# Value pages spread between past sums, later stores and states, a second home for the last value pages, and 4+4 output weight tiles in a hybrid decoder kernel

## The chip, the cores and the metric

The kernel runs as one launch on one core of a Trainium2 chip. TensorE (PE in the profile) multiplies and transposes, VectorE (DVE), ScalarE (ACT) and GpSimd (POOL) compute, and SyncE (SP) and GpSimd issue most of the transfers, which 16 DMA engines carry out. The metric is the device time of one execution in microseconds (us). Each engine runs its own instructions in the order written, and engines wait for each other through semaphores.

## The reference

Two layers over 256 prompt tokens and 64 sample tokens (8 sequences of 8 new tokens, each with 1024 past tokens in a paged cache of 128-token pages). The model width is 1024.

```python
def trunk(x, sample):
    for l in range(DEPTH):                       # 2 layers
        x = x + 0.5 * _swiglu(_rmsnorm(x, norm_ffn1_g[l]), ffn1_w_gate[l], ffn1_w_up[l], ffn1_w_down[l])
        o, rows = _token_mix(_rmsnorm(x, norm_mix_g[l]), w_in[l], ..., w_out[l], past)
        x = x + o
        x = x + 0.5 * _swiglu(_rmsnorm(x, norm_ffn2_g[l]), ffn2_w_gate[l], ffn2_w_up[l], ffn2_w_down[l])
    return _rmsnorm(x, norm_final_g)

def _token_mix(h, ...):
    qa, ka, va, qf, kf, vf, ff, qc, fc, ic, gc = jnp.split(h @ w_in, split_at, axis=-1)
    oa = _moba_attend(qa, ka_all, va_all, pos0)          # 6 heads: 256-key blocks, each query keeps its best 3
    of = _fox_attend(qf, kf_all, vf_all, lf_all, pos0)   # 5 heads: score + sum of log forget gates between
    oc, s_new = _hgrn2_recurrence(qc, kc, ic, logf_c, s0)    # 5 heads: linear recurrence with a state
    oc = _rmsnorm(oc, hgrn_g) * jax.nn.silu(heads(gc, C_HEADS))
    o = jnp.concatenate([oa, of, oc], axis=-1) @ w_out
```

The outputs are the new x, and for every layer the new keys, values, forget logs and states.

## The kernel before

All 320 tokens lie in the columns of the tiles. A layer goes through five stages: FFN1, input projection, a mix loop, the output projection and FFN2. In the dense stages (`dense`, PE line L1647) each float32 weight tile is split in two: ACT writes the high part (`hi`, L644), DVE the rest (`lo`, L956), and PE forms three products, x high by w high, x high by w low, x low by w high. Weights come into two raw buffers, "slots" 0 and 1, in turn.

The mix loop has 32 iterations a layer, i = 4q+n, one for each 256-key block n (two pages) of each sequence q. In iteration i, PE transposes the keys of block i+1 (`turn_keys`, L1864, 12 transposes into three PSUM banks that ACT and DVE copy out by turns) and multiplies block i's scores (`block_scores`, L1886). Once per sequence it adds, for the sequence before: at n=1 the transposed softmax weights (L1897, L1901), at n=2 the weighted values (`values`, L1913 to L1921), and at n=3 a transpose of their result (`turn_outputs`, L1929). In the gaps lie the prompt's own attention (i up to some 15), the levels of the recurrence (i=15 to 23) and from i=24 on (END0) its ends, states and root mean squares. After the loop stand these three steps for the last sequence, q=7.

Four queues feed the loop, each in a written order:

- SP loads key pages (two transfers a page, L510 and L511, four page slots that PE frees in turn), the recurrence's states (`load_states`, three transfers, L526) and stores new tokens (`store_tokens`, L519 and L520).
- POOL loads value pages (`load_values`, two transfers a page, L615 and L616), eight pages a sequence into one buffer, each once the sequence before has used that page. Between them it does `add_past` (L608), a copy of the summed forget logs behind the keys of a block; `turn_keys` of that block waits for it.
- ACT: copies of the key transposes (L778), exponentials (L788), softmax factors and scaled weights (`block_factors`, L804 to L815), copies of turned weights (L824), and in iteration 29 the recurrence's root mean squares (`rec_rstd`, L875 and L878, an Ln and an Exp, each with an ACT_TABLE_LOAD ahead). `block_factors` of q=0 waits for all ten stores of the new tokens.
- DVE: row maxima and gates (L1318 to L1330), key copies, norms, scaled outputs (`scale_outputs`, L1360), their copies into the mixed rows (`copy_outputs`, L1369 to L1372) and the recurrence.

The output projection takes its eight k-tiles in four chunk pairs, slot 0 with five tiles and slot 1 with three. ACT (hi), DVE (lo) and PE each wait for the one before them. After each pair DVE adds the product into x (`accumulate`), squares it (L970), adds the square up (L971) and forms the low part of the next x. Ahead of it, PE waits for `ol` (L1616), the low part of the mixed sample rows, which DVE forms behind `lo(0)` of the first chunk.

Of the kernel before, what the change touches and what calls it, by code (L numbers as in the profile page):

```python
# [33 lines left out]
ALU = mybir.AluOpType  # L34
# [219 lines left out]
def trunk(nc, a, outs):  # L254
    ctx = ExitStack()
    with ctx:
# [40 lines left out]
        value_pages = sb("value_pages", [128, NPG, AW + BW])  # L297
        sb("value_rest", [128, 18 * NT - NPG * (AW + BW)])
# [5 lines left out]
        pt = lambda n: P[:, n * NT:(n + 1) * NT]  # L304
        ROW_AT = [384 * n for n in (0, 2, 1, 3, 4)]
# [109 lines left out]
        out_tok, out_st = sem("out_tok"), sem("out_state")  # L415
# [22 lines left out]
        def _(sp):  # L438
# [21 lines left out]
            def wout_chunks(L, m):  # L460
# [3 lines left out]
                fill(0, u, [(raw[0][:, 0:5, :], rows(0, 640).rearrange("l (k p) n -> p (l k) n", p=128))])  # L464
                sp.wait_ge(split_done[1], u + 1)
                sp.dma_start(raw[1][0:64, 0, :], rows(640, 64).rearrange("l p n -> (l p) n")).then_inc(wout_in, 16)
                fill(1, u, [(raw[1][64:128, 0, :], rows(960, 64).rearrange("l p n -> (l p) n")),
                            (raw[1][:, 1:3, :], rows(704, 256).rearrange("l (k p) n -> p (l k) n", p=128))])
# [10 lines left out]
            for L in range(DEPTH):  # L479
# [33 lines left out]
                def store_tokens(groups):  # L513

                    for g in groups:
# [3 lines left out]
                        sp.dma_start(pv[:, ds(L * 2, 2), :], tokp[:, 0:2, g * 384:g * 384 + w]).then_inc(out_tok, 16)  # L519
                        sp.dma_start(sv[ds(L, 1), :, :].rearrange("l t c -> (l t) c"), toks[0:NS, g * 384:g * 384 + w]).then_inc(out_tok, 16)  # L520
# [12 lines left out]
                store_tokens(KEY_OUTS)  # L533
                sp.dma_start(outs["fox_logf_prompt"].rearrange("l b (n p) h -> p (l b n) h", p=128)[:, ds(L * 2, 2), :],
                             tokf[:, 0:2, :]).then_inc(out_tok, 16)
                sp.dma_start(outs["fox_logf_sample"].rearrange("l b t h -> l (b t) h")[ds(L, 1), :, :].rearrange("l t h -> (l t) h"),
                             tokf[0:NS, 2, :]).then_inc(out_tok, 16)
                for pg in range(6):
                    key_page(0, pg)
                load_states()  # L540
                sp.wait_ge(rows_copied_dve, L * 8 + 6)
                sp.wait_ge(rows_copied_act, L * 7 + 6)
                for pg, g in zip((6, 7), VALUE_OUTS):
                    key_page(0, pg)
                    store_tokens((g,))
                for q in range(1, DB):
                    for pg in range(NPG):
                        key_page(q, pg)

# [27 lines left out]
            sp.wait_ge(out_tok, 10 * 16 * DEPTH)  # L577
# [6 lines left out]
        def _(pool):  # L584
# [13 lines left out]
            for L in range(DEPTH):  # L598
# [1580 lines left out]
```

## Time and profile before

| | us |
|---|---|
| median of three runs | 1723.29 (1721.86 to 1725.35) |
| the profiled execution | 1721.82 |
| its span in the trace | 1720.1 |
| PE busy | 1608.1 (93%) |
| DVE busy | 1059.7 (62%) |
| ACT busy | 666.5 (39%) |

In the trace a layer's mix loop stands at 366 to 596 and 1207 to 1438 us, its output projection at 596 to 632 and 1438 to 1474. The number after a row's start is how long it took, xN counts the instructions put together in it, and brackets name the idle time before it and what ended that. PEclk is the granted clock of PE as a share of full speed.

### The profile page before, as it was taken

How to read it: one execution, taken by the hardware profiler on the slowest of the kernel's cores; microseconds unless marked ns; L12 is line 12 of the kernel's file. 1: busy time of each engine (PE TensorE's matmuls, PEld its weight loads, DVE VectorE, ACT ScalarE, POOL GpSimd, SP SyncE). 2: the span in 40 equal slices, each digit the busy share in tenths (PEclk: the TensorE clock that was granted, in tenths of full speed). 3: DMA queues.
4: the chain of work that ended last, by engine and by line, in shares of the span. 5: the costliest groups of instructions: out<-in, count | busy, mean ns of one | idle time of the engine just before them, and what ended most of it. 6: DMA issues, size and time to landing. Idle time of an engine off the chain costs nothing. (4 is left out here: it accounts for less than half of the span.)

```text
span 1720.1 us, 35333 instructions
## 1 busy us (share of the span) xinstructions
PE 1608.1 (93%) x13333; PEld 1492.0 (87%) x13333; DVE 1059.7 (62%) x1800; ACT 666.5 (39%) x969; POOL 160.6 (9%) x329
## 2 busy tenths in 40 slices
PE   6999999979989689999999999999799887999998
PEld 6999999966666489999999999999567666999997
DVE  6666557646576476665566665666556755766654
ACT  4333332436453443333343333425554442433323
POOL 0000000022424200000000000000233431000000
PEclk9999999989999799999999999999898997999999
DMA  6544455556757444444444444554766773544444
GB/s 199 155 154 153 136 152 131 147 188 206 236 180 242 146 147 147 146 147 139 154 156 153 153 141 143 157 143 121 226 211 206 218 216 120 170 153 150 140 141 141
DMA packets 282107, 282.34 MB, mean 164 GB/s; under 512 B 42894, under 2 KB 270918, under 8 KB 281862
## 3 DMA queue, kind: packets, MB, share of 16 engines
q1 hardware_dynamic: 266210, 234.28, 44.8%
q0 software_dynamic: 14464, 46.48, 8.5%
q8 instruction: 72, 1.18, 0.3%
q14 instruction: 45, 0.37, 0.1%
q10 hardware_dynamic: 1316, 0.03, 0.1%
HBM read 274.34 MB, written 6.40 MB: 163 GB/s over the span
## 5 line engine op out<-in xcount | busy, mean ns | idle before, releaser
L1647 PE MATMUL PS<-xh,whi 128*128 128x320 f32 x1840 | 576.0, 313 | 12.7 <-DVE xl L965 7.0
L1647 PE MATMUL PS<-xl,whi 128*128 128x320 f32 x1840 | 569.2, 309 | 0.0
L1647 PE MATMUL PS<-xh,wlo 128*128 128x320 f32 x1840 | 569.2, 309 | 0.0
L644 ACT ACTIVATE whi<-raw 128x2048 fp32r<-128x2048 f32 (+2 forms) x181 | 331.1, 1829 | 571.5 <-PE PS L1647 566.9
L956 DVE TENSOR_TENSOR wlo<-raw,whi 128x2048 fp32r<-128x2048 f32 (+2 forms) x181 | 395.3, 2184 | 235.2 <-ACT whi L644 233.0
L1647 PEld LDWEIGHTS PS<-xh,whi 128*128 128x128 f32 x1840 | 346.1, 188 | 15.9 <-DVE wlo L956 10.1
L1647 PEld LDWEIGHTS PS<-xh,wlo 128*128 128x128 f32 x1840 | 346.1, 188 | 1.5
L1647 PEld LDWEIGHTS PS<-xl,whi 128*128 128x128 f32 x1840 | 345.9, 188 | 0.0
L1647 PE MATMUL PS<-hh,whi 128*128 128x320 f32 x704 | 217.7, 309 | 0.0
L1647 PE MATMUL PS<-hl,whi 128*128 128x320 f32 x704 | 217.5, 309 | 0.0
L1647 PE MATMUL PS<-hh,wlo 128*128 128x320 f32 x704 | 217.5, 309 | 0.0
L1864 PE MATMUL PS<-K,key_pages 128*128 128x128 f32 x768 | 114.5, 302 | 50.7 <-POOL key_pages L608 21.5
L1864 PEld LDWEIGHTS PS<-K,key_pages 128*128 128x128 f32 x768 | 94.4, 155 | 65.9 <-issue 63.0
L778 ACT ACTIVATE keys_t<-PS 128x512 f32<-128x512 f32 x128 | 75.1, 595 | 151.8 <-PE PS L1864 151.7
L1647 PEld LDWEIGHTS PS<-hh,wlo 128*128 128x128 f32 x704 | 132.1, 188 | 0.0
L1647 PEld LDWEIGHTS PS<-hh,whi 128*128 128x128 f32 x704 | 132.1, 188 | 0.0
L1647 PEld LDWEIGHTS PS<-hl,whi 128*128 128x128 f32 x704 | 132.1, 188 | 0.0
L608 POOL COPY key_pages<-past 128x10 f32<-128x10 f32 x64 | 15.7, 250 | 1099.6 <-DVEq L951 953.6
L999 DVE TENSOR_TENSOR tmp<-PS,rstd 128x320 f32<-128x320 f32 x88 | 42.5, 487 | 88.8 <-PE PS L1647 88.7
L1303 DVE COPY keys_t<-PS 128x512 f32<-128x512 f32 x64 | 44.2, 691 | 76.0 <-PE PS L1864 72.3
L664 ACT ACTIVATE tmp<-tmp 128x320 f32<-128x320 f32 x88 | 40.3, 463 | 117.2 <-DVE tmp L999 117.1
L615 POOL DMA_DIRECT2D value_pages<-in_cache_moba_v x128 | 70.1, 547 | 151.7 <-issue 94.8
(262 smaller groups left out, 1793.6 us busy)
## 6 DMA issues: line engine op xcount, KB each, us to landing
raw<-in_ffn_w_gate SPq DMA_DIRECT2D x45, 1024.0 KB
raw<-in_ffn_w_up SPq DMA_DIRECT2D x45, 1024.0 KB
raw<-in_ffn_w_down SPq DMA_DIRECT2D x32, 1024.0 KB
key_pages<-in_cache_moba_k SPq DMA_DIRECT2D x128, 192.0 KB, 2.8
value_pages<-in_cache_moba_v POOLq DMA_DIRECT2D x128, 192.0 KB, 3.2
raw<-in_w_in SPq DMA_DIRECT2D x46, 512.0 KB
key_pages<-in_cache_fox_k SPq DMA_DIRECT2D x128, 160.0 KB, 3.5
value_pages<-in_cache_fox_v POOLq DMA_DIRECT2D x128, 160.0 KB, 3.8
```

Of the source, the lines that this page charges most:

```text
L608: pool.tensor_copy(key_pages[:, pg:pg + 2, AW + BW:AW + BW + BH], past_of[:, L, q, 2 * n:2 * n + 2, :]).then_inc(past_in, 1)
L615: pool.dma_start(value_pages[:, pg, 0:AW], vmv[:, ds(page + L * NPOOL, 1), :].rearrange("p a c -> p (a c)")).then_inc(v_in[pg], 16)
L644: act.activation(whi[s][:, 0:nk, 0:w], raw[s][:, 0:nk, 0:w], ACT.Copy).then_inc(hi_done[s], 1)
L664: act.activation(tmp[j][:, :], tmp[j][:, :], ACT.Silu).then_inc(silu_done, 1)
L778: act.activation(keys_t[i % 2][:, 4 * u:4 * u + 4, :], PS[:, bank, :].rearrange("p (j c) -> p j c", j=4), ACT.Copy).then_inc(read_act[bank ...
L956: dve.tensor_tensor(wlo[s][:, 0:nk, 0:w], raw[s][:, 0:nk, 0:w], whi[s][:, 0:nk, 0:w].bitcast(F32), ALU.subtract).then_inc(split_done[s], 1)
L999: dve.tensor_tensor(tmp[j][:, :], PS[:, j, 0:NT], rstd[:, :], ALU.mult).then_inc(gate_scaled, 1)
L1303: dve.tensor_copy(keys_t[i % 2][:, 4 * u:4 * u + 4, :], PS[:, bank, :].rearrange("p (j c) -> p j c", j=4)).then_inc(read_dve[bank], 1)
L1647: last = te.matmul(out, w[wslot][r, kt, cols], x[r, at, :], start=start and n == 0 and m == 0, stop=stop and n == len(ktiles) - 1 and m == 2)
L1864: last = te.transpose(PS[:, bank, 128 * j:128 * j + 128], key_pages[:, pg % 4, 128 * pr:128 * pr + 128], ident)
```

## The change

- **Value pages.** Those of sequence 0 are loaded one, one, two, two and two at a time, with a past sum between them; before, all eight stood ahead of the third past sum. The last sequence's pages 0 to 4 go to a second home, `late_pages`, in the rows of P that the prompt's scores no longer need, and are loaded in sequence 6 (three in iteration 24, two in 25); pages 5 to 7 stay where they were.
- **SP.** Sequence 0's key pages go through without a store or state between them; the value stores stand behind the fourth and the eighth page of sequence 1, the states behind the fourth page of sequence 3. The stores' semaphore is split, and `block_factors` of q=0 waits for the six key and forget stores alone.
- **ACT.** In iteration 29 the three banks with mean squares are copied first; Ln and Exp (and their two table loads) stand after the copies of the turned weights.
- **DVE.** `copy_outputs(q-1)` moves to the end of the iteration in which its transpose is made, one iteration earlier. Behind the loop, `prompt_out_lo` (L1555 before) moves behind the weight copies, and both `lo` of the first output chunk before `scale_outputs(7)`.
- **Output projection.** Four and four k-tiles per slot; squares are made by ACT and added by DVE; `lo(1)` of the next pair stands between the two accumulates.

```diff
+        late_pages = P[:, 0:LATE * (AW + BW)].rearrange("p (n c) -> p n c", n=LATE)
...
-                fill(0, u, [(raw[0][:, 0:5, :], rows(0, 640).rearrange("l (k p) n -> p (l k) n", p=128))])
+                fill(0, u, [(raw[0][:, 0:4, :], tiles(0, 512))])
...
-                for pg in range(6):
+                for pg in range(NPG):
                     key_page(0, pg)
-                load_states()
-                sp.wait_ge(rows_copied_dve, L * 8 + 6)
-                sp.wait_ge(rows_copied_act, L * 7 + 6)
-                for pg, g in zip((6, 7), VALUE_OUTS):
-                    key_page(0, pg)
-                    store_tokens((g,))
                 for q in range(1, DB):
                     for pg in range(NPG):
                         key_page(q, pg)
+                        if q == 1 and pg % 4 == 3:
...
+                            store_tokens((VALUE_OUTS[pg // 4],), out_tok)
+                        if (q, pg) == (3, 3):
+                            load_states()
...
+                def load_late_values(first, count):
+
+                    pool.wait_ge(prompt_scores_ready, (L + 1) * NH)
+                    for pg in range(first, first + count):
+                        load_page(DB - 1, pg, late_pages[:, pg, :], late_v_in[pg])
...
-                load_values(0, 0)
-                load_values(0, 1)
+                for i, first, count in ((2, 0, 1), (3, 1, 1), (4, 2, 2), (5, 4, 2)):
+                    load_values(0, first, count)
+                    add_past(i)
+                load_values(0, 6, 2)
                 pool.memset(a_blocks[:, :, :], 0.0).then_inc(products_cleared, 1)
-                add_past(2)
                 for i in range(BLOCKS):
                     q, n = divmod(i, NBLK)
-                    if i + 3 < BLOCKS:
+                    if 6 <= i + 3 < BLOCKS:
                         add_past(i + 3)
-                    if n >= 2 and q >= 1:
-                        load_values(q, n - 2)
+                    if n >= 2 and 1 <= q < DB - 1:
+                        load_values(q, 4 * (n - 2), 4)
+                    if n < 2 and q == DB - 2:
+                        load_late_values(3 * n, 3 - n)
+                    if n == 2 and q == DB - 1:
+                        load_values(q, LATE, NPG - LATE)
...
                     if q == 0:
-                        act.wait_ge(out_tok, (L + 1) * 160)
+                        act.wait_ge(out_keys, (L + 1) * 96)
...
                     if i == END0 + 5:
-                        rec_rstd()
+                        copy_mean_squares()
...
+                    if i == END0 + 5:
+                        rec_rstd()
...
-                    if n == 0 and q >= 2:
-                        copy_outputs(q - 2)
...
+                    if n == 3 and 1 <= q < DB - 1:
+                        copy_outputs(q - 1)
                 q = DB - 1
                 block_stats(BLOCKS - 1)
                 gates(q)
-                prompt_out_lo()
                 copy_outputs(q - 1)
                 norms(q)
                 copy_weights(q)
+                prompt_out_lo()
+                lo(0, L * USES + OFF["wout"], 4)
+                lo(1, L * USES + OFF["wout"], 4)
                 scale_outputs(q)
                 copy_outputs(q)
-                lo(0, L * USES + OFF["wout"], 5)
...
-                    lo(1, u, 3)
-                    lo(0, u + 1, 5 if p < 3 else 8)
-                    accumulate(L * 3 + 2, p, 1.0, 1, u, (xh, xl))
+                    lo(0, u + 1, 4 if p < 3 else 8)
+                    accumulate(L * 3 + 2, p, 1.0, 1, u, (xh, xl), L * KT_D, (lambda: lo(1, u + 1, 4)) if p < 3 else None)
```

POOL at the start of a layer's loop: a past sum is the COPY into `key_pages`, a page is a TENSOR_LOAD of its number and two transfers (DMA). Before, after the first two past sums (the rows from the second page to the eighth are left out between the two pieces):

```order
L608 COPY key_pages<-past 128x2x5 x2
L614 TENSOR_LOAD pages
L614 ISA x2
L615 ISA
L615 DMA value_pages<-in_cache_moba_v 128x384
L616 ISA
L616 DMA value_pages<-in_cache_fox_v 128x320
```

```order
L616 DMA value_pages<-in_cache_fox_v 128x320
L624 MEMSET idle 128x1280
L608 COPY key_pages<-past 128x2x5 x8
```

Now, at the same place:

```order
L614 COPY key_pages<-past 128x2x5 x2
L618 TENSOR_LOAD pages
L618 ISA x2
L619 ISA
L619 DMA value_pages<-in_cache_moba_v 128x384
L620 ISA
L620 DMA value_pages<-in_cache_fox_v 128x320
L614 COPY key_pages<-past 128x2x5
```

The third past sum stood behind eight pages and a memset; now it stands behind one page, and the memset behind the sixth past sum.

DVE at the end of the loop, from the last copy of turned weights on. Before (the low part of the prompt's rows, `ol` 128x8x256, stands above this piece, right behind the last gates):

```order
L1351 COPY weight_cols<-PS 64x112
L1360 TENSOR_SCALAR idle<-PS,row_stats 112x256
L1369 COPY P<-PS 64x4x8
L1370 COPY P<-PS 64x4x8
L1371 COPY P<-PS 64x2x8
L1372 COPY P<-PS 64x8
L956 TENSOR_TENSOR wlo<-raw,whi 128x1280
L1616 TENSOR_TENSOR ol<-P,oh 128x8x64
```

Now:

```order
L1396 COPY weight_cols<-PS 64x112
L1600 TENSOR_TENSOR ol<-P,oh 128x8x256
L990 TENSOR_TENSOR wlo<-raw,whi 128x1024 x2
L1405 TENSOR_SCALAR idle<-PS,row_stats 112x256
L1414 COPY P<-PS 64x4x8
L1415 COPY P<-PS 64x4x8
L1416 COPY P<-PS 64x2x8
L1417 COPY P<-PS 64x8
L1662 TENSOR_TENSOR ol<-P,oh 128x8x64
```

The low part of the prompt's rows went behind the copies of the weights, and the low weights (`wlo`) no longer stand between the last copy of outputs and the low part of the sample rows (`ol` 128x8x64).

ACT in iteration 29. Before:

```order
L815 ACTIVATE toks<-new_row_all,factors 112x64
L875 ACT_TABLE_LOAD
L875 ACTIVATE b<-PS,K 128x320 x3
L878 ACT_TABLE_LOAD
L878 ACTIVATE b<-b 128x960
L778 ACTIVATE keys_t<-PS 128x512 x2
```

Now:

```order
L836 ACTIVATE toks<-new_row_all,factors 112x64
L896 ACTIVATE b<-PS 128x320 x3
L799 ACTIVATE keys_t<-PS 128x512 x2
L809 ACTIVATE weight_rows,exp_sums<-PS,minus_max 112x256
L845 ACTIVATE weight_cols<-PS 128x448
L902 ACT_TABLE_LOAD
L902 ACTIVATE b<-b,K 128x960
L903 ACT_TABLE_LOAD
L903 ACTIVATE b<-b 128x960
L799 ACTIVATE keys_t<-PS 128x512 x2
```

The two table loads went from ahead of block 30's key copies to ahead of block 31's.

## Rows read from the trace of the kernel before

**Rows 1.** Stretches: start:end, length, PE, PEld, DVE, ACT, POOL busy, PEclk, DMA share, GB/s.

```profile
366.00:596.00 230.00, 189.72 (x2537) 138.60 (x2535) 139.36 (x382) 111.37 (x289) 78.58 (x159) 0.90 0.68 212
596.00:632.00 36.00, 31.69 (x192) 30.39 (x192) 21.71 (x32) 11.32 (x13) 0.00 (x0) 0.93 0.47 146
632.00:1207.00 575.00, 573.24 (x3900) 569.53 (x3900) 356.50 (x462) 205.55 (x174) 0.34 (x2) 1.00 0.48 146
```

**Rows 2.** Waits of PE, both layers: total us, times, longest us.

```profile
PE PS L1864 <- POOL key_pages L608: 21.5, 2, 11.1
PE PS L1864 <- DVE P L1372: 13.6, 10, 3.6
PE PS L1647 <- DVE wlo L956: 10.9, 11, 2.6
PE PS L1647 <- DVE ol L1616: 7.2, 2, 3.6
PE PS L1913 <- DMA value_pages<-in_cache_fox_v: 6.8, 7, 1.7
...
PE PS L1864 <- ACT b L875: 5.5, 2, 2.8
```

**Rows 3.** POOL at the start of layer 0's loop.

```profile
366.39 0.60 POOL L615 DMA_DIRECT2D value_pages<-in_cache_moba_v  x1 [11.74 <-issue]
...
381.32 0.34 POOL L608 COPY key_pages<-past 128x10 f32<-128x10 f32 x2
```

**Rows 4.** PE at the loop's start, two blocks of layer 0 and one of layer 1.

```profile
381.68 2.79 PE L1864 MATMUL PS<-K,key_pages 128*128 128x128 f32 x12 [11.11 <-POOL key_pages L608]
...
394.02 1.47 PE L1864 MATMUL PS<-K,key_pages 128*128 128x128 f32 x12
...
1222.52 2.79 PE L1864 MATMUL PS<-K,key_pages 128*128 128x128 f32 x12 [10.40 <-POOL key_pages L608]
```

**Rows 5.** DMA: size and landing of a key page's two halves, rates at 366 to 384 and 448 to 452.

```profile
key_pages<-in_cache_moba_k SPq DMA_DIRECT2D x128, 192.0 KB, 2.8
key_pages<-in_cache_fox_k SPq DMA_DIRECT2D x128, 160.0 KB, 3.5
...
DMA packets 5183, 5.14 MB, mean 286 GB/s; under 512 B 3474, under 2 KB 4564, under 8 KB 5182
...
448.00:452.00 4.00, 3.71 (x35) 2.48 (x36) 2.45 (x8) 2.84 (x9) 2.69 (x6) 1.00 1.01 351
```

**Rows 6.** SP's queue: the states, and around page 3 of sequence 3.

```profile
369.90 4.35 SPq L526 DMA_DIRECT2D states<-in_state_hgrn  x3
...
436.61 0.78 SPq L511 DMA_DIRECT2D key_pages<-in_cache_fox_k  x1
444.34 0.33 SPq L510 DMA_DIRECT2D key_pages<-in_cache_moba_k  x1
```

**Rows 7.** ACT in iterations 29 to 31 of layer 0.

```profile
559.72 1.28 ACT L875 ACT_TABLE_LOAD   x1
...
564.68 1.07 ACT L778 ACTIVATE keys_t<-PS 128x512 f32<-128x512 f32 x2
...
575.65 0.30 ACT L804 ACTIVATE factors<-masked_max,row_stats 112x5 f32<-112x5 f32 x1 [0.32 <-DVE row_stats L1330]
```

**Rows 8.** PE from the last values to the first matmul of FFN2, layer 0.

```profile
580.46 0.65 PE L1913 MATMUL PS<-value_pages,weight_cols 128*32 128x128 f32 x8 [0.92 <-DVE weight_cols L1348]
...
589.30 0.65 PE L1913 MATMUL PS<-value_pages,weight_cols 128*32 128x128 f32 x8 [0.84 <-DMA value_pages<-in_cache_fox_v]
...
595.85 0.63 PE L1647 MATMUL PS<-oh,whi 128*128 128x320 f32 x1 [3.60 <-DVE ol L1616]
...
632.24 0.42 PE L1647 MATMUL PS<-xh,whi 128*128 128x320 f32 x1 [1.89 <-DVE wlo L956]
```

**Rows 9.** DVE and ACT ahead of the output projection, layer 0.

```profile
593.26 1.49 DVE L956 TENSOR_TENSOR wlo<-raw,whi 128x1280 fp32r<-128x1280 f32 x1 [0.17 <-DVE P L1372]
...
593.21 0.63 ACT L924 ACTIVATE oh<-P 128x512 fp32r<-128x512 f32 x1 [13.27 <-DVEq L951]
```

More of the change, by code:

```diff
@@ L414, in trunk @@
         first_squares_ready, first_squares_added = sem("first_squares_ready"), sem("first_squares_added")
-        out_tok, out_st = sem("out_tok"), sem("out_state")
+        out_tok, out_keys, out_st = sem("out_tok"), sem("out_keys"), sem("out_state")
+        late_v_in = [sem(f"late_v_in{j}") for j in range(LATE)]
+        squares_ready, squares_added = sem("squares_ready"), sem("squares_added")
         block = ctx.enter_context(nc.Block())
@@ L979, in accumulate @@
                     dve.wait_ge(acc_used, 4 + (w - 1) * KT_D + k + 1)
-                    if j == 0:
+                    if j == 1 and between is not None:
+                        between()
+                    if j == 0 and squared is None:
                         square(k)
@@ L989, in accumulate @@
                         dve.tensor_scalar(xt(k), xt(k), gains[:, w * 8 + k:w * 8 + k + 1], None, ALU.mult).then_inc(y_scaled, 1)
-                    if j == 1 and w < DEPTH * 3:
+                    if squared is not None:
+                        add_square(squared + k)
+                    elif j == 1 and w < DEPTH * 3:
                         square(k)
@@ L1910, in values @@
                     for pg in range(NPG):
-                        te.wait_ge(v_in[pg], Q * 32 + 32)
+                        late = q == DB - 1 and pg < LATE
+                        page = (late_pages if late else value_pages)[:, pg, :]
+                        if late:
+                            te.wait_ge(late_v_in[pg], (L + 1) * 32)
+                        else:
+                            te.wait_ge(v_in[pg], (L * (DB - 1 if pg < LATE else DB) + q + 1) * 32)
                         for g, c in enumerate(GROUP_PAIR):
-                            te.matmul(PS[groups[g], bank, 0:128], weight_cols[:, pg, groups[g]], value_pages[:, pg, c:c + 128], start=pg == 0, stop=False, skip_group_check=True)
+                            te.matmul(PS[groups[g], bank, 0:128], weight_cols[:, pg, groups[g]], page[:, c:c + 128], start=pg == 0, stop=False, skip_group_check=True)
                         for g, (c, to) in enumerate(GROUP_REST):
-                            last = te.matmul(PS[groups[g], bank, to:to + 64], weight_cols[:, pg, groups[g]], value_pages[:, pg, c:c + 64], start=False, stop=False, skip_group_check=True)
+                            last = te.matmul(PS[groups[g], bank, to:to + 64], weight_cols[:, pg, groups[g]], page[:, c:c + 64], start=False, stop=False, skip_group_check=True)
                         last.then_inc(values_used, 1)
```

71 lines of the change are left out of this document (46 added, 25 removed).

## The prediction

> **What bounds the kernel now.** I read the stretches first [rows 1]. In the dense stages PE has no idle time to speak of (573.24 us busy of 575 in the long one, 573.24/3900 = 0.147 us a matmul), and nothing in the change touches them. The mix loop and the output projection are where PE idles: of 230 us it is busy for 189.72, at a granted clock of 0.90, and of the projection's 36 for 31.69. DVE (139 us) and ACT (111 us) are far from full there, so no engine bounds the loop as a whole; single waits do. So the second view is PE's waits [rows 2], with two entries per kind where a wait occurs once a layer: the largest is one wait a layer for the third past sum on POOL (21.5 us together), then ten waits for `copy_outputs` (13.6), the low weights (10.9, in every stage), `ol` (7.2), the last value pages (6.8) and `rec_rstd` (5.5). The timelines tell where each stands [rows 3, 4, 7 to 9], and the DMA rows what the transfers have left [rows 5]. The part of PE's clock matters as well: after 11.11 us of idling the first twelve transposes took 2.79 us, at half of the speed of 1.47 that the same twelve take a few blocks later [rows 4]; that is the lower of the clock's two levels, 1.2 instead of 2.4 GHz.
>
> **The sum, part by part, both layers together.** It is made against the profiled execution, 1721.82 us, 1.5 below the median.
>
> *Past sums between value pages.* POOL issues sixteen transfers from 366.39 and reaches the third past sum at 381.32 [rows 3], about 15 us for eight pages and a memset, or some 1.75 a page. With one page ahead of it the sum is there at about 368.5, before PE has done the block ahead. That removes 11.11 + 10.40 us of waiting and the slow restart, 2 x (2.79 - 1.47) = 2.6: 24.1 us. It is not all gain, for what is late next are the key pages themselves. From 366.4 on, the loop needs eight more key pages (blocks 2 to 5) while POOL sends for eight value pages: sixteen pages of 192 + 160 KB, 5.77 MB. The queues moved 286 GB/s in this crowd and 351 in a crowded stretch of the loop [rows 5]. At 286 they take 20.2 us and end at 386.6, at 351 they take 16.4 and end at 382.8; block 5's transposes began at 394.02 [rows 4]. So by the lower rate a layer gains 7.4 us, by the higher 11.2, 15 to 22 for both. The states and two pairs of stores that shared the lower rate are gone from this stretch, which speaks for the higher one. I take **18**.
>
> The Trainium skill's page "DMA: Bandwidth & Descriptors" says (section "Queues, rings and completion order") that every DMA engine takes turns between the queues it has work for, packet by packet, so value pages on POOL's queue slow key pages on SP's even when they are issued in a better order; its specifications name about 358 GB/s as one core's limit from HBM. By that figure the sixteen pages take 16.1 us (an estimate from that page), ending at 382.5, which would make this term 23 instead of 18. The trace's 286 in the crowd is below the limit, its 351 just under it.
>
> *The last value pages.* Once PE starts the last values at 580.46 it waits for four of the eight pages, the last at 589.30 [rows 8]; seven such waits of both layers make 6.8 us [rows 2]. Pages 0 to 4 now come during sequence 6, four iterations earlier. Pages 5 to 7 are the first of POOL's queue instead of the last, five pages of 1.75 us or 8.8 us earlier, so that the last lands before 581, while PE reaches it after five pages or more. Gain **6.8**; the bounds are 3 (if the first of the three is still late) and 7.5 (with faster restarts).
>
> *`ol` without `lo(0)` ahead.* DVE's `lo(0)` runs from 593.26 for 1.49 us and `ol` behind it, while ACT's copy that `ol` needs is done at 593.21 + 0.63 [rows 9]. `ol` can start 0.8 earlier: **1.5** for two layers. The moved `lo` and `prompt_out_lo` go into DVE's wait for the last values, at which PE works from 580.46 till after 589.30 [rows 8].
>
> *4+4 tiles.* From 595.85 to FFN2's first matmul at 632.24 are 36.39 us [rows 8]. 192 matmuls at 0.147 are 28.2; the clock of 0.93 over 36 us adds 2.5 [rows 1]; the wait of 1.89 at the end is for FFN2's weights, which the change leaves alone. That is a floor of 32.6, and so at most 3.8 a layer. With equal chunks each low part takes DVE 1.49 x 4/5 = 1.2 us [rows 9] behind 24 matmuls of 3.5, and the squaring leaves DVE, so that the waits inside go nearly to nothing: **6.5** of 7.6. The new cost is on ACT, two squares a pair, each of fewer columns than the 0.63 us copy [rows 9], while it was busy 11.32 us of 36 [rows 1]: nothing, hidden behind PE's matmuls.
>
> *`copy_outputs` one iteration earlier.* Its waits are 13.6 us, the longest 3.6 [rows 2]. They arise when the copies stand behind other work on DVE while PE wants their bank. Put at the end of the iteration before, they are in time unless DVE itself is late, which it sometimes is while the recurrence's levels run. Bounds 0 and 13.6; I take 60 %, **8**.
>
> *`rec_rstd`.* PE's waits for it are 5.5 us [rows 2]. They go, but the same table loads, Ln and Exp stand ahead of block 31's key copies instead of block 30's: from 559.72 to 564.68 ACT spends 5 us on it now [rows 7], of which only the reading of the three banks stays in front. The wait moves by an iteration, and DVE's `rec_outputs` and the last gates behind it come later; the last factors at 575.65 [rows 7] may slip by some tenths. I book **0**; bounds -3 and +5.5.
>
> *Costs.* Five late pages come in iterations 24 and 25, where nothing came before: 1.8 MB a layer, 5.1 us at 351 GB/s if it delayed PE one for one, nothing if hidden in a loop whose mean is 212 GB/s [rows 1, 5]. On SP the states take 4.35 us and stand where SP waits about 7 us for a free slot, from 436.61 + 0.78 to 444.34 [rows 6]; two pairs of stores stand ahead of key pages of sequence 2, which delays them by a store's issue each. Bounds 0 and 10.2; nearer to hidden: **-4**.
>
> The sum is 18 + 6.8 + 1.5 + 6.5 + 8 + 0 - 4 = 36.8 us. 1721.8 - 36.8 = 1685.0 for a profiled execution, and 1.5 more, 1686, for the median.
>
> **Rivals.** *Key pages take the place of the past sum* (chance 0.15). The crowd stays as slow as 286 GB/s or slower, and waits for key pages of some 8 us a layer replace the wait for the sum: the first term is 6 and not 18, and the time 1698. For it speaks the rate of [rows 5], against it that the states and two pairs of stores leave the stretch. The page on DMA named above would have it so wherever both queues are full.
>
> *DVE sets the pace of the loop* (0.13). The copies are as late as before and `rec_rstd` costs 3: 36.8 - 8 - 3 = 25.8, time 1697. For it speak the levels of the recurrence, against it 139 us of 230.
>
> *The late home doesn't do its work* (0.08): pages 5 to 7 or the late ones land as late as before, since POOL holds them back. Then 6.8 becomes 2 and the time is 1691.
>
> *Everything comes through* (0.17). The higher rate holds, the copies' waits vanish, no cost shows: 22 + 6.8 + 1.5 + 7.6 + 13.6 = 51.5, time 1672.
>
> *Slower* (0.03): the light blocks of the loop become bound by transfers. Half of a key page lands 3.5 us after its issue [rows 5]; if the spread value pages, late pages and stores make it later than PE's slack in every block, by more than 36.8/64 = 0.6 us a block, nothing is left, and at 1 us it is 27 us slower, 1750. For that the loop's mean rate would have to fall, and 212 GB/s is far below the 351 shown. A change that does nothing is not to be seen: the order shows every move.
>
> **How the numbers follow.** My forecast, the sum as it stands, has 0.44 and gives 1686 us, by its own bounds 1676 to 1695. The range takes in the rivals of 1672, 1691, 1697 and 1698 with a margin of 4: 1668 to 1702, and leaves out the slower case and the bounds meeting on one side. A measurement of this kernel tells 0.2 %, some 3.4 us, from no change. The gain has to shrink by over 33 us to be lost in that: faster 0.95, same 0.02, slower 0.03.
>
> **What the profile after would show.** The wait for past sums gone from PE's list, and in its place waits for key pages of less than 5 us a layer. No wait for value pages at the end of the loop, and 3 us less from the first of the last values to the output projection, beside the 0.8 of `ol`. The projection's stage at 33 us. `copy_outputs` under 6 us. The wait for `rec_rstd` in another iteration. The prediction is wrong if the key pages' waits are over 12 us, if waits for DVE or ACT in the loop grow by what the others lose, or if the later states and stores hold up SP.

## The result and the profile after

The changed kernel takes 1698.28 us (median of four runs, 1694.7 to 1707.67) against 1722.57 of the kernel before: a ratio of 0.9861, interval 0.9834 to 0.9887. It is 24 us faster, where 37 were forecast. The profiled execution has a span of 1699.0 us, 21.1 less than before.

The stretches of the mix loop and of the output projection, layer by layer (columns as in [rows 1]):

```profile
368.00:591.00 223.00, 194.30 (x2539) 142.35 (x2538) 141.23 (x382) 112.61 (x290) 79.31 (x159) 0.91 0.71 223
591.00:627.00 36.00, 34.28 (x213) 33.79 (x213) 19.78 (x30) 15.17 (x23) 0.00 (x0) 0.92 0.41 134
1198.50:1421.00 222.50, 195.49 (x2538) 143.20 (x2536) 140.87 (x382) 112.61 (x290) 79.70 (x159) 0.90 0.71 223
```

PE's waits, which answer to [rows 2]:

```profile
PE PS L1909 <- DMA key_pages<-in_cache_fox_k: 9.6, 9, 2.8
...
PE PS L1692 <- DVE wlo L990: 5.9, 3, 2.5
PE PS L1692 <- DVE ol L1662: 5.6, 2, 2.8
...
PE PS L1963 <- ACT keys_t L799: 5.4, 2, 2.8
...
PE PS L1909 <- DVE tmp L1460: 2.8, 2, 1.4
...
PE PS L1909 <- ACT b L896: 2.5, 2, 1.2
```

Gone are the past sums (21.5), the copies of outputs (13.6) and the last value pages (6.8); the low weights and `ol` are shorter. New are 9.6 us for key pages (0.9 before) and 5.4 for key copies on ACT, ahead of the values of sequence 6. The whole list went from 105 to 79 us and the span down by 21. PE at the start of layer 0's loop shows a part of it:

```profile
370.84 1.06 PE L1931 MATMUL PS<-keys_t,qz 128*32 128x256 f32 x16
...
376.76 1.54 PE L1909 MATMUL PS<-K,key_pages 128*128 128x128 f32 x6 [2.84 <-DMA key_pages<-in_cache_fox_k]
378.23 1.93 PE L1931 MATMUL PS<-keys_t,qz 128*32 128x256 f32 x16
380.09 1.65 PE L1991 MATMUL PS<-P 64*128 64x128 f32 x4
381.67 2.82 PE L1909 MATMUL PS<-K,key_pages 128*128 128x128 f32 x12
...
386.65 1.53 PE L1909 MATMUL PS<-K,key_pages 128*128 128x128 f32 x12
```

The second half of a key page is 2.84 us late, and behind that wait PE runs at half speed (twelve transposes in 2.82 us against 1.53 a block later), for some 9 us. In [rows 4] there was one wait of 11 us with the same kind of restart; now there is a short wait with a restart that lasts longer.

To see where the gain stands, I take the times of the blocks' scores in both traces (score of block 0 as the start) and add the stages behind the loop. Gain of the change in us:

| stretch | layer 0 | layer 1 | both | forecast |
|---|---|---|---|---|
| score of block 0 to block 5 | 5.5 | 6.3 | 11.8 | 18 |
| block 5 to 15 | -3.3 | -5.0 | -8.3 | -4 |
| block 15 to 28 | 0.5 | 3.7 | 4.2 | 8 |
| block 28 to 31 | -1.8 | -1.4 | -3.2 | 0 |
| last values to the output projection | 5.5 | 4.2 | 9.7 | 6.8 + 1.5 |
| output projection to FFN2 | 3.5 | 3.7 | 7.2 | 6.5 |

The sum is 21.4, the span's gain 21.1. The stretches that the table leaves out come to -0.4: block 0's score of layer 0 is 2.2 us later than before, and 1.8 us are gained between the last score and the last values and in the dense stages. What stands behind the loop was worth what was forecast and a little more; inside the loop 26 - 4 was forecast and 4.5 was got.

### The profile page after: what moved, and what is told of

It reads as the page before. It is cut to its first block and busy times, and to the rows that moved or that the text cites. A ratio compares the mean times of both kernels' runs of the same rounds, so it can differ in the third digit from the quotient of the medians.

```text
span 1699.0 us, 35356 instructions
## 1 busy us (share of the span) xinstructions
PE 1612.7 (95%) x13333; PEld 1498.6 (88%) x13333; DVE 1053.1 (62%) x1784; ACT 674.4 (40%) x987; POOL 162.4 (10%) x329
## 5 line engine op out<-in xcount | busy, mean ns | idle before, releaser
L665 ACT ACTIVATE whi<-raw 128x2048 fp32r<-128x2048 f32 (+1 forms) x181 | 330.9, 1829 | 567.2 <-PE PS L1692 561.4
L990 DVE TENSOR_TENSOR wlo<-raw,whi 128x2048 fp32r<-128x2048 f32 (+1 forms) x181 | 395.1, 2184 | 237.8 <-ACT whi L665 236.3
L1909 PEld LDWEIGHTS PS<-K,key_pages 128*128 128x128 f32 x768 | 96.1, 157 | 44.4 <-issue 30.6
L619 POOL DMA_DIRECT2D value_pages<-in_cache_moba_v x118 | 64.5, 547 | 148.0 <-issue 89.0
```

The costliest lines, as they stand in the source:

```text
L619: pool.dma_start(to[:, 0:AW], vmv[:, ds(page + L * NPOOL, 1), :].rearrange("p a c -> p (a c)")).then_inc(landed, 16)
L665: act.activation(whi[s][:, 0:nk, 0:w], raw[s][:, 0:nk, 0:w], ACT.Copy).then_inc(hi_done[s], 1)
L990: dve.tensor_tensor(wlo[s][:, 0:nk, 0:w], raw[s][:, 0:nk, 0:w], whi[s][:, 0:nk, 0:w].bitcast(F32), ALU.subtract).then_inc(split_done[s], 1)
L1909: last = te.transpose(PS[:, bank, 128 * j:128 * j + 128], key_pages[:, pg % 4, 128 * pr:128 * pr + 128], ident)
```

## The experiments

All but one start from the changed kernel and undo or move one thing. Each is judged by its ratio to the kernel before on the same chip, set against the change's 0.9861, and by the times of the blocks' scores in its trace. The kernel before itself differs between the four groups of runs (medians of 1722.57, 1724.73, 1727.58 and 1726.51 us), so the medians of two groups are not subtracted; 0.001 of the ratio is 1.7 us, and the difference of two ratios is known to some 5 to 8 us either way.

**The start: the spread and SP's order, each alone.** `front_before` puts POOL's old order back:

```diff
-                for i, first, count in ((2, 0, 1), (3, 1, 1), (4, 2, 2), (5, 4, 2)):
-                    load_values(0, first, count)
-                    add_past(i)
-                load_values(0, 6, 2)
+                load_values(0, 0, 8)
                 pool.memset(a_blocks[:, :, :], 0.0).then_inc(products_cleared, 1)
+                add_past(2)
...
```

> The changed kernel with all eight value pages of sequence 0 and the memset ahead of the third past sum again. Theory one (what is gained at the start stays until the end of the loop): the wait of some 11 us a layer for the past sum comes back, the score of block 1 is 8 us later, that of block 5 about 5.5 to 6.5, and the end of the loop as much: the time is 10 to 13 us higher, 1708 to 1711. Rival (the light blocks behind it run up against key pages, and the gain is lost there): block 15's score is only 1 to 2 us later and the time 2 to 4 us higher, 1700 to 1702.

Measured 1710.59 us (1703.72 to 1710.91), 0.9918 of the kernel before (0.9901 to 0.9934): 10 us of the gain are lost. `sp_before` puts the states and the value stores back among sequence 0's key pages:

```diff
-                for pg in range(NPG):
+                for pg in range(6):
                     key_page(0, pg)
+                load_states()
...
+                for pg, g in zip((6, 7), VALUE_OUTS):
+                    key_page(0, pg)
+                    store_tokens((g,), out_tok)
...
```

> The changed kernel with the states and the value stores back among sequence 0's key pages on SP. Theory one (what stands there delays the pages of blocks 2 and 3, which now are wanted at once): a wait for key pages of 4 to 6 us a layer at block 3 in place of one under 1, block 5 some 3 to 5 us later, the clock low there longer, the time 6 to 10 us higher than the changed kernel beside it. Rival (the first waits are for pages that SP has issued already, and the later states cost as much in the middle): within 3 us of it.

Measured 1707.94 us (1702.5 to 1708.43), 0.9883 (0.9855 to 0.9911). The changed kernel run beside it (`after_again`, below) has 1700.54 us and 0.986: 7 us less by the medians, 4 by the ratios, whose intervals overlap. `spread_alone` is the kernel before with POOL's new order and nothing else:

```diff
-                load_values(0, 0)
-                load_values(0, 1)
+                for i, first, count in ((2, 0, 1), (3, 1, 1), (4, 2, 2), (5, 4, 2)):
+                    load_some(0, first, count)
+                    add_past(i)
+                load_some(0, 6, 2)
                 pool.memset(a_blocks[:, :, :], 0.0).then_inc(products_cleared, 1)
-                add_past(2)
...
```

> The kernel before with one edit: sequence 0's value pages issued one, one, two, two, two between the past sums. Theory one (the wait for past sums goes, but states and stores still stand between SP's key pages, and the copies of outputs still stall PE later): block 1 comes 8 us earlier, block 5 only 2 to 4 us, and the time is 2 to 6 us under that of the kernel before. Rival (the spread alone makes the whole gain at the start): block 5 comes 5.5 us earlier and the time is 10 to 13 us lower.

Measured 1724.29 us (ten runs), 0.999 (0.9971 to 1.0008): nothing. Here are the stretches from the score of block 0 to that of block 5 in layer 0, of the kernel before, of `spread_alone`, `front_before`, `sp_before` and of the change, one fence each:

```profile
368.66:400.00 31.34, 20.23 (x172) 13.46 (x171) 15.10 (x46) 15.04 (x44) 9.34 (x21) 0.78 0.87 276
```

```profile
368.54:399.53 30.99, 21.39 (x171) 13.71 (x170) 15.29 (x46) 15.15 (x44) 9.45 (x20) 0.83 0.91 279
```

```profile
369.09:400.67 31.58, 20.54 (x172) 13.69 (x171) 15.11 (x46) 15.16 (x44) 9.37 (x21) 0.78 0.70 227
```

```profile
370.12:402.56 32.44, 26.00 (x171) 16.13 (x171) 15.46 (x46) 15.15 (x44) 9.48 (x20) 0.68 0.87 268
```

```profile
370.84:396.69 25.85, 22.56 (x171) 14.46 (x170) 15.61 (x46) 15.15 (x44) 9.54 (x20) 0.80 0.90 287
```

The first five blocks take 31.3, 31.0, 31.6, 32.4 and 25.9 us (31.4, 30.4, 30.5, 30.5 and 25.1 in layer 1). Either part alone gives 1 us or nothing; together they give 5.5 to 6.3 a layer. The wait only changes its name when the spread stands alone; PE's waits of `spread_alone`:

```profile
PE PS L1869 <- DMA key_pages<-in_cache_fox_k: 16.6, 9, 3.7
PE PS L1869 <- DVE P L1377: 14.6, 10, 3.6
```

16.6 us for key pages, all in the first five blocks of the two layers, stand where 21.5 for past sums were: this is the rival that key pages take the place of the past sum, in a kernel that had only that part of the change. In `sp_before` PE is busy for 26.00 us of the same 171 matmuls at a clock of 0.68, against 20 to 22.6: waits of 2.70, 1.14 and 1.94 us in a row, for the keys of blocks 2 and 3, cost more here, with the clock behind them, than one of 11. In layer 1 its first five blocks take 30.5 us, less than the 31.4 of the kernel before.

**`copy_outputs` back in the next iteration** (`copy_before`):

```diff
-                    if n == 3 and 1 <= q < DB - 1:
-                        copy_outputs(q - 1)
...
+                    if n == 0 and q >= 2:
+                        copy_outputs(q - 2)
```

> The changed kernel with the copies of outputs back in the iteration after. Theory one (as predicted, a part of the 13.6 us of waits came off the end): the waits for the copies come back, 11 to 14 us, and the time is 4 to 8 us higher, 1702 to 1706. Rival (the loop's middle is paced by something else, so the wait only changed its name): the waits come back and waits for the weights' copies and the levels shrink by as much, the time is within 2 us of 1698.

Measured 1710.68 us (1705.37 to 1716.52), 0.9907 (0.9885 to 0.993): 8 us lost, the upper end of theory one. The waits come back as forecast, 12.5 us. From the score of block 15 to that of block 28 in layer 0, first `copy_before`, then the change:

```profile
464.94:563.35 98.41, 87.19 (x1175) 65.74 (x1174) 68.10 (x169) 39.36 (x99) 41.21 (x82) 0.86 0.69 224
```

```profile
463.50:555.65 92.15, 81.73 (x1174) 62.27 (x1174) 68.01 (x169) 39.39 (x99) 41.80 (x82) 0.93 0.73 238
```

Of the 6.3 us of difference, 5.5 are PE's own busy time: the same matmuls, at a clock of 0.86 and not 0.93. Its idle time is nearly the same, 11.2 against 10.4 us: without the copies' waits others stand there, up to 2.1 us each, for turned weights and levels. In layer 1 the same stretch takes 96.1 us against 92.5, and PE's busy time alone is 4.1 us longer, at 0.88 against 0.93. The trace is that of the slowest of the four runs (1716.52 us).

**The root mean squares as before** (`rec_before`) **and one block later still** (`rec_late`):

```diff
                     if i == END0 + 5:
-                        copy_mean_squares()
+                        rec_rstd()
...
-                    if i == END0 + 5:
-                        rec_rstd()
```

> The changed kernel with the root mean squares of the recurrence put back as they were: Ln and Exp with their table loads ahead of block 30's key copies. Theory one (the move costs more at block 31 than it gives at block 30): the wait ahead of block 30's keys grows from 1.25 to 2.8 us a layer, the wait of the values of sequence 6 for the key copies of block 31 (2.7 us) goes, and the score of block 31 comes 1.4 to 1.8 us a layer earlier; the time is some 3 us lower, 1695. Rival (the move gives what the waits of the kernel before promise): the time is 3 to 5 us higher, 1702.

Measured 1692.97 us (1688.19 to 1696.26), 0.9821 (0.9805 to 0.9838): 7 us less than the change. In the change, ACT does this in iteration 29, and PE waits behind it:

```profile
563.40 1.28 ACT L902 ACT_TABLE_LOAD   x1
564.69 1.09 ACT L902 ACTIVATE b<-b,K 128x960 f32<-128x960 f32 x1
565.81 1.28 ACT L903 ACT_TABLE_LOAD   x1
567.10 1.00 ACT L903 ACTIVATE b<-b 128x960 f32<-128x960 f32 x1
568.01 1.06 ACT L799 ACTIVATE keys_t<-PS 128x512 f32<-128x512 f32 x2
```

```profile
568.84 0.42 PE L1963 MATMUL PS<-value_pages,weight_cols 128*32 128x128 f32 x8 [2.67 <-ACT keys_t L799]
```

The values of sequence 6 want the PSUM bank that ACT's key copies of block 31 read from 568.01 on, and these stand behind 4.6 us of table loads, Ln and Exp. `rec_late` has them behind all key copies, the recurrence's outputs on DVE behind the last gates, and the high part of the prompt's rows on ACT behind the last copies of weights:

```diff
-                    if i == END0 + 5:
+                    if i == END0 + 6:
                         rec_rstd()
...
                 gates(q)
                 copy_outputs(q - 1)
+                rec_outputs()
                 norms(q)
...
```

> The changed kernel with Ln and Exp of the root mean squares one block later still, behind all key copies, the recurrence's outputs on DVE behind the last gates, and the high part of the prompt's rows behind the last copies of weights. Theory one (table loads, Ln and Exp cost only where key copies stand behind them): no wait for the key copies of block 31 (2.7 us a layer before) and none for block 30 beyond 1.3, the last factors some 2.3 us a layer earlier, of which 0.6 goes to DVE's outputs: 3 to 5 us faster, 1693 to 1695. Rival (DVE's work behind the last gates becomes the end of the chain): the last copy of weights comes as late as now, or later, 1698 to 1702.

Measured 1691.4 us (1688.48 to 1694.76), 0.9805 (0.9765 to 0.9844): under the change, and not clear of `rec_before`. From the score of block 28 to that of block 31 the change takes 18.1 us in layer 0, the kernel before 16.3, `rec_before` 16.6 and `rec_late` 13.5; `rec_late` gives 0.8 back ahead of the last values, where PE waits longer for DVE's copy of the weights:

```profile
573.05 0.65 PE L1961 MATMUL PS<-P,weight_cols 128*32 128x128 f32 x8 [1.81 <-DVE weight_cols L1392]
```

**The last value pages in their first home** (`late_before`):

```diff
-                    if n >= 2 and 1 <= q < DB - 1:
+                    if n >= 2 and q >= 1:
                         load_values(q, 4 * (n - 2), 4)
-                    if n < 2 and q == DB - 2:
-                        load_late_values(3 * n, 3 - n)
-                    if n == 2 and q == DB - 1:
-                        load_values(q, LATE, NPG - LATE)
...
```

> The changed kernel with all eight value pages of sequence 7 in their first home, loaded at sequence 7. Theory one (the term of the last value pages as predicted): waits for value pages of 6 to 7 us come back at the end of the loop, the time is 7 to 9 us higher, 1705 to 1707, and the first loads of the late pages never cost anything in iterations 24 and 25. Rival (the late pages cost in the loop what they give at its end): the score of block 31 comes 2 to 4 us a layer earlier and the time is within 3 us of 1698.

Measured 1706.51 us (1704.15 to 1711.02), 0.9894 (0.9854 to 0.9935): by the ratios 6 us lost, which the intervals do not set clear of nothing. The trace does: the waits for value pages are back with 9.2 us, and from the first of the last values to the output projection it takes 16.0 and 15.4 us in the two layers, against 9.9 and 9.3 in the change.

```profile
577.31 0.65 PE L1959 MATMUL PS<-value_pages,weight_cols 128*32 128x128 f32 x8 [0.91 <-DVE weight_cols L1392]
...
593.35 0.63 PE L1688 MATMUL PS<-oh,whi 128*128 128x320 f32 x1 [2.81 <-DVE ol L1658]
```

From block 15 to block 28 it takes 93.4 us in layer 0 against 92.2, and 91.9 against 92.5 in layer 1: the late pages cost the loop nothing that could be seen.

**The output projection as before** (`wout_before`, with `lo(0)` behind the last copies of outputs again):

```diff
-                kts = [(k, k, ALLR) for k in range(4)]
+                kts = [(k, k, ALLR) for k in range(5)]
...
-                kts = [(k, 4 + k, ALLR) for k in range(4)]
+                kts = [(0, 5, ALLR), (1, 6, ALLR), (2, 7, ALLR)]
...
```

> The changed kernel with the output projection of the kernel before: five and three k-tiles, squares on DVE, and the first low weights behind the last copies of outputs (so that the 0.8 us a layer ahead of the projection is given back too). Theory one: the stage grows from about 32.6 to 36.3 us and the wait ahead of it from 2.8 to 3.6, 9 us for both layers, 1707. Rival (the stage is held by FFN2's weights, which come late anyway): the stage grows inside and the wait for FFN2's first weights shrinks by as much, 1700 to 1702.

Measured 1704.44 us (1703.32 to 1708.71), 0.9883 (0.9845 to 0.9922): by the ratios 4 us lost, not clear of nothing. In the trace it is 8: its stage takes 35.5 and 36.0 us and the wait ahead of it 3.76 and 3.60, against 32.9 and 32.5 and twice 2.81 in the change. In the change, layer 0:

```profile
580.96 0.65 PE L1963 MATMUL PS<-P,weight_cols 128*32 128x128 f32 x8 [1.00 <-DVE weight_cols L1396]
...
590.82 0.63 PE L1692 MATMUL PS<-oh,whi 128*128 128x320 f32 x1 [2.81 <-DVE ol L1662]
...
623.69 0.41 PE L1692 MATMUL PS<-xh,whi 128*128 128x320 f32 x1 [1.72 <-DVE wlo L990]
```

From 590.82 to 623.69 are 32.9 us, against the floor of 32.6 that the prediction worked out, and the one wait left in it is FFN2's, as expected there.

**Value pages spread evenly over all blocks** (`even`):

```diff
+                    add_past(i)
                     load_values(0, first, count)
-                    add_past(i)
...
+                    if i == 4:
+                        load_values(0, 6, 2)
+                    if n >= 2 and 1 <= q < DB - 1:
+                        load_values(q, *((0, 3), (3, 2))[n - 2])
+                    if n < 2 and q >= 2:
+                        load_values(q - 1, *((5, 2), (7, 1))[n])
...
-                    if n >= 2 and 1 <= q < DB - 1:
-                        load_values(q, 4 * (n - 2), 4)
```

> The changed kernel with value pages issued more evenly: each past sum of sequence 0 ahead of the pages instead of behind them, its last two pages one block later, and every later sequence's eight pages as three, two, two and one over four blocks instead of four and four over two. Theory one (value pages in bursts make key pages late, 9.6 us of waits and slow restarts behind them): the waits for key pages fall under 4 us and the time by 5 to 8, to 1690 to 1693. Rival (in the blocks where this happens the next wait stands right behind): the waits for key pages fall, others grow, the time stays within 2 us of 1698.

A miss: 1711.43 us (1702.74 to 1717.01), 0.9914 (0.9881 to 0.9948), slower than the change. The waits for key pages rose from 9.6 to 15.9 us, and value pages of later sequences came late, 4.2 us in two waits. That value pages which are spread out meet more key pages is a reading of these waits; no run shows it by itself.

**Fewer value pages at the very start** (`rec_before_thin`, with the root mean squares as before, the memset ahead of the past sums and the value stores at sequence 4):

```diff
-                for i, first, count in ((2, 0, 1), (3, 1, 1), (4, 2, 2), (5, 4, 2)):
+                for i, first, count in ((2, 0, 0), (3, 0, 0), (4, 0, 1), (5, 1, 1), (6, 2, 2), (7, 4, 2)):
                     load_values(0, first, count)
                     add_past(i)
...
-                        if q == 1 and pg % 4 == 3:
+                        if q == 4 and pg % 4 == 3:
```

> The changed kernel with the root mean squares as they were before, no value page ahead of the third and fourth past sums (one ahead of the fifth and of the sixth, two ahead of the seventh and of the eighth, then the last two), and the value stores moved to sequence 4. Theory one (the first key pages wait because value pages of the same moment share the DMA engines with them): the waits for key pages in the first four blocks fall from 3.1 and 2.9 us a layer to under 1, no clock drop there, and the time is 4 to 8 us under that of the kernel with the root mean squares as before, 1685 to 1689. Rival (the first key pages need their 4 us from issue to landing anyway): the waits stay over 2 us a layer and the time at 1691 to 1694.

Measured 1690.21 us (1687.41 to 1695.61), 0.9803 (0.9761 to 0.9844). In layer 0 the waits for key pages in the first blocks fall to 0.7 us and less, and the score of block 5 comes after 21.7 us instead of 25.5. The ratio is 0.002 under that of `rec_before`, less than the four us asked for and within both intervals: the start is better, the whole is not shown to be by this run.

**Both together** (`rec_late_thin`), and **the change once more** (`after_again`), on one chip:

> The changed kernel with both improvements: Ln and Exp behind all key copies as in the run rec_late, and the thinner value pages at the start with the stores at sequence 4 as in the run rec_before_thin. Theory one (the two stand in different places and add): 3 to 5 us under the lower of the two, 0.977 to 0.980 of the kernel before, 1686 to 1689. Rival (the clock and the key pages of the light blocks level it out): 0.980 to 0.983, no better than either.

> The changed kernel once more, on the chip and in the hours of the three beside it. Its first median was 1698.28 (1694.7 to 1707.67). Theory one (undoing the parts one by one gave back 12 + 12 + 8 + 6 - 5 = 33 us of a gain of 24, because the first four runs drew a low clock on the way): it comes out at 0.981 to 0.985 of the kernel before. Rival (the parts overlap, so that each is worth more with the others there): 0.986 again.

`after_again` took 1700.54 us (1693.2 to 1703.82), 0.986 (0.9834 to 0.9886), as at first. `rec_late_thin` took 1685.23 us (1679.62 to 1691.64), 0.9757 (0.973 to 0.9783), the lowest of all and clear of the change, though not of `rec_late` and `rec_before_thin`: that the two improvements add is not shown by the times. Its first five blocks in layer 0, and block 28 to 31:

```profile
370.21:392.06 21.85, 19.35 (x171) 12.06 (x170) 15.17 (x46) 15.72 (x45) 9.90 (x21) 1.00 0.93 302
...
549.57:563.12 13.55, 11.91 (x214) 8.81 (x213) 5.13 (x14) 10.88 (x26) 0.82 (x3) 1.00 0.74 208
```

21.85 us at a full clock and 302 GB/s, against 25.85 at 0.80 and 287 in the change; 13.55 against 18.08. In layer 1 the end is as short (13.55 against 18.01), while the start gains only 0.5. `after_again` gave the number of its second theory, 0.986. The puzzle that both theories were to solve, parts that give back 33 us of a gain of 24, came from subtracting the medians of different groups of runs. By the ratios the same five runs give back 10 + 8 + 6 + 4 - 7 = 21 us, so an overlap of the parts is not shown by it.

## Why the prediction was right, and by how much not

The direction and the range were right, the size was not: 24 us against 36.8. The noise was taken too small as well: not 0.2 % but 13 us lie between the four runs of the change, and the interval of its ratio is 0.27 % either way. By its own steps:

- **Past sums between value pages: 18 forecast, 11.8 measured up to block 5.** The mechanism was right, and so was the doubt that key pages come late next; the size came from the wrong quantity. The step that was mis-sized is "sixteen pages of 192 + 160 KB, 5.77 MB ... I take 18": it priced the volume up to block 5 at a rate, as if all the pages were sent without a pause. The rate was the lower of its two (287 GB/s in the stretch), at which its own sum gives 15. But SP sends a key page only into a slot that PE has freed, and from 366 to 397 us it waits for PE six times, 11.9 us in all:

```profile
SPq L514 <- PE PS L1909: 11.9, 6, 5.8
```

```profile
371.71 0.33 SPq L516 DMA_DIRECT2D key_pages<-in_cache_fox_k  x1
...
378.20 0.33 SPq L515 DMA_DIRECT2D key_pages<-in_cache_moba_k  x1
...
385.99 0.33 SPq L515 DMA_DIRECT2D key_pages<-in_cache_moba_k  x1
```

  The page half sent at 371.71 is the one that PE gets at 376.76, 5.0 us later, while POOL sends value pages that are wanted four blocks later. Block 4's pages leave SP from 378.20 on, and block 5's last page at 385.99, when by the sum at its higher rate all sixteen had landed. From 376.76 on PE hardly waits (0.16 us up to block 5); it is slow. The prediction counted the slow restart as saved (2.6 us), while the new, shorter wait has a restart of its own, at a granted clock of 0.53 over 9 us. That the order of the pages counts is shown by `rec_before_thin` and `rec_late_thin`: with value pages sent later the wait at block 2 falls to 0.7 or 0.8 us in layer 0, and the stretch gains 3.8 to 4.0 us more (0.5 to 4.3 in layer 1). The stores that these two runs also move go out at 386.94 and 395.37 in the change, too late to cause that wait. `rec_before_thin` gains 9.6 us up to block 5 in either layer, so the 18 were there to be had.
- **That this gain is the spread's** is not so. Neither the spread nor SP's order gives anything alone (31.0 and 31.6 against 31.3 us); the two waits lay over each other, and what the prediction mentioned in half a sentence (states and stores leave the stretch) is needed as much as the spread. Put back, either part costs the whole of this gain in the traces: 62.0 and 62.9 us for both layers, against 50.9 in the change and 62.8 before. In this the parts do overlap. The times are too coarse to show more: by the ratios the six parts, undone one by one, give back 10 + 4 + 8 + 6 + 4 - 7 = 25 us of a gain of 24, each known to some 5 to 8 us.
- **The light blocks: -8.3 against a cost of 4** that was to cover the late pages too. In layer 0 PE waits 2.2 us for key pages between the scores of blocks 12 and 13, with a slow restart, while POOL sends the eight value pages of sequence 3 without a break. In layer 1 the waits are under 0.7 us, and the loss is clock: 66.41 us busy at 0.92, against 61.12 at 1.00 before.

```profile
1241.63:1303.82 62.19, 61.12 (x802) 43.05 (x801) 36.20 (x119) 34.83 (x102) 21.86 (x47) 1.00 0.70 218
```

```profile
1226.35:1293.54 67.19, 66.41 (x802) 46.72 (x801) 36.31 (x119) 34.82 (x102) 22.32 (x48) 0.92 0.72 225
```

  In the trace of `after_again` the same stretch loses 2.5 us at 0.97 and 0.97, so that some 6 of the 8.3 belong to one execution. What would remove the rest stays open: in `even`, where the bursts are spread, the stretch takes 64.1 and 67.4 us, no less than the 62.4 to 67.2 of the two traces of the change.
- **`copy_outputs`: 8 forecast, 4.2 between the traces of before and after, 8 by undoing it.** The size is met by undoing it, and partly by luck: the waits went entirely, not by 60 %, and waits for turned weights and levels took part of their place. The price of such a wait was taken as its length, where in the trace of `copy_before` the loss is mostly PE's own time at a lower clock.
- **`rec_rstd`: booked at 0, measured -3.2 in the trace (-1.7 in that of `after_again`), and -7 by undoing it.** The bound of -3 was there. The step that failed is "the wait moves by an iteration": 1.25 us of it stay ahead of block 30, and 2.67 us are new at a place where PE waited for nothing before, ahead of the values of sequence 6, since the 4.6 us of table loads, Ln and Exp now stand before both of ACT's copies of block 31.
- **The last value pages and `ol`: 8.3 forecast, 9.7 measured.** Right in place and size; PE waits for no value page there, and put back, the pages cost 12.3 us at this place in the trace.
- **4+4 tiles: 6.5 forecast, 7.2 measured.** Right; the floor of 32.6 us was met within 0.3.
- **The cost of the late pages**, the other part of the 4, is not seen in the blocks where they land.

The rival "key pages take the place of the past sum" gave 1698, which is the measured time, but its price was not what happened: the first term was 11.8 and not 6, and the rest was lost at three other places. It did happen in full in `spread_alone`. The Trainium skill's "DMA: Bandwidth & Descriptors" says (section "Queues, rings and completion order") that the queues share the engines packet by packet. The traces agree as to the sharing, in that value pages issued on POOL's queue made key pages on SP's late (a wait of 2.84 us in the change, 0.7 where the value pages come later); the turns by packet no run here shows. The limit of 358 GB/s that the same page of the Trainium skill names in its specifications, by which the term would have been 23 us (an estimate from that page), was not reached: the stretch moved 287.

## What to carry to other kernels

A wait that two queues cause together goes only when both are changed; before pricing one of them, ask what the other would release at, and try each alone. A short wait is not priced at its length: where the clock falls behind it, the same matmuls cost more for blocks to come, and a change that turns one long wait into three short ones can lose. Where a queue may send only into slots that the reader frees, its pages are priced by when they are released and how long each takes to land, not by volume over rate. Runs of different groups are compared by their ratios to a common kernel beside them, not by their medians. When a step is moved out of the way of one reader, look who stands behind the place where it goes, on that engine, and move it behind the last of them.

## What was not expected of the hardware

- The granted clock fell behind a wait of 2.84 us (key pages, block 2 of the change: the next twelve transposes took 2.82 us) and rose again some 9 us later. In the kernel before, the wait for the root mean squares was 2.76 us in layer 0 and 2.77 in layer 1 [rows 2], and the twelve transposes behind it took 1.50 us, full speed, in one and 1.86 in the other. The length of one wait alone does not tell.

```profile
561.84 1.50 PE L1864 MATMUL PS<-K,key_pages 128*128 128x128 f32 x12 [2.76 <-ACT b L875]
...
1405.63 1.86 PE L1864 MATMUL PS<-K,key_pages 128*128 128x128 f32 x12 [2.77 <-ACT b L875]
```

- It also fell with no wait at all. In layer 1 of the change, with PE busy throughout, it was 0.66 for these 5 us, behind a run of small matmuls (5*128 and 64*128 in the rows), and the twelve transposes in them took 2.55 us:

```profile
1258.00:1263.00 5.00, 5.00 (x25) 3.59 (x29) 1.21 (x3) 1.15 (x3) 0.04 (x1) 0.66 0.14 49
```

```profile
1260.35 2.55 PE L1909 MATMUL PS<-K,key_pages 128*128 128x128 f32 x12
```

  A like run of small matmuls from 1249.58 on was followed by transposes in 1.53 us. What makes the difference stays open.
- One kernel's time varies together with the clock it is granted: the four runs of the change have spans of 1693.0, 1694.2, 1699.0 and 1706.0 us at mean clocks of 0.975, 0.974, 0.970 and 0.966. The median clock of the change is 0.972 in these runs and 0.970 in the five of `after_again`, that of the kernel before 0.965 in the seventeen beside those. By the slope of the four spans (13 us for 0.009) a difference of 0.005 is worth 7 us, an estimate of the clock's part in the 24; it cannot tell clock lost behind a wait from clock lost without one.
- An Ln followed by an Exp had a table load of 1.28 us ahead of each, with no idle time beside it.
